# A decoder layer on one core: first weight halves in quarters, retention queries and keys from x without its norm, x through ScalarE's queue

## What is computed

```python
h = rms_norm(x, attn_norm)                       # x * rsqrt(mean(x*x)) * gain
q_r, k_r, v_r, g_r, q_m, k_m, v_m = split(h @ w_in)
qr, kr = rotary(q_r, pos), rotary(k_r, pos)      # cos and sin per position and channel
o_r = retention_chunkwise(qr, kr, v_r)           # scores * decay, then values
... # group norm, MoBA attention, gates, output projection, residual, norm, gated MLP with a convolution
```

## Time and profile before

| | us |
|---|---|
| median of 3 runs (lowest, highest) | 477.55 (477.21, 477.62) |
| the profiled execution | 477.05 |
| its span, first to last instruction | 475.3 |
| TensorE busy in it | 468.3 |
| VectorE busy in it | 300.1 |
| ScalarE busy in it | 254.4 |

### The profile page before, as it was taken

One profiled execution on the slowest core, in us unless ns is written; L12 is line 12 of the kernel. 1 busy time (PEld: TensorE's weight loads), 2 busy tenths in 40 slices (PEclk: granted clock), 3 DMA queues, 4 the chain that ended last, 5 costly groups with the idle time before them and its releaser, 6 DMA issues.

```text
span 475.3 us, 7781 instructions
## 1 busy us (share of the span) xinstructions
PE 468.3 (99%) x3117; PEld 431.4 (91%) x3117; DVE 300.1 (63%) x364; ACT 254.4 (54%) x362; POOL 19.6 (4%) x27
## 2 busy tenths in 40 slices
PE   7999999999999999999999999999999999999997
PEld 5789999888888999999999888999999999988885
DVE  4787882755664637355338676687777878885312
ACT  5774432147774849224445355776666666663400
POOL 0300000311110001000000000000000000000000
DMA  8997444254445525753443733615554555538002
GB/s 299 413 375 266 178 177 179 90 182 166 150 147 220 199 88 178 311 177 134 157 188 122 267 145 132 248 67 223 187 185 189 183 193 187 196 123 329 1 1 88
DMA packets 13979, 87.20 MB, mean 183 GB/s; under 512 B 1537, under 2 KB 1921, under 8 KB 4353
## 3 DMA queue, kind: packets, MB, share of 16 engines
q1 hardware_dynamic: 13536, 85.25, 48.0%
q0 software_dynamic: 416, 1.57, 0.8%
HBM read 85.77 MB, written 1.05 MB: 183 GB/s over the span
## 4 chain that ended last, share of the span: by engine, by line
PE 94%; DMA 3%; SPq 1%; POOL 1%; issue 0%; DVE 0%; ACT 0%; POOLq 0%
PE bank L365 18%; PE bank L366 18%; PE bank L367 18%; PE bank L331 5%; PE bank L329 5%; PE bank L330 5%; PE bank L601 4%; PE bank L602 4%; PE bank L604 4%; DMA ys<-x_dram 3%; PE bank L518 2%; PE bank L520 2%; PE bank L519 2%; PE bank L384 2%; PE bank L467 1%; PE bank L449 1%
## 5 line engine op out<-in xcount | busy, mean ns | idle before, releaser
L900 DVE TENSOR_TENSOR w_lo<-w_raw,w_hi 128x2048 fp32r<-128x2048 f32 x75 | 170.4, 2288 | 78.7 <-ACT w_hi L624 78.4
L365 PE MATMUL bank<-h_hi,w_hi 128*128 128x256 f32 x576 | 163.8, 284 | 0.0
L366 PE MATMUL bank<-h_lo,w_hi 128*128 128x256 f32 x576 | 163.0, 283 | 0.0
L367 PE MATMUL bank<-h_hi,w_lo 128*128 128x256 f32 x576 | 163.0, 283 | 0.0
L624 ACT ACTIVATE w_hi<-w_raw 128x2048 fp32r<-128x2048 f32 x75 | 141.7, 1914 | 31.5 <-PE bank L604 16.9
L365 PEld LDWEIGHTS bank<-h_hi,w_hi 128*128 128x128 f32 x576 | 110.5, 192 | 0.5 <-issue 0.4
L366 PEld LDWEIGHTS bank<-h_lo,w_hi 128*128 128x128 f32 x576 | 110.6, 192 | 0.1
L367 PEld LDWEIGHTS bank<-h_hi,w_lo 128*128 128x128 f32 x576 | 110.5, 192 | 0.0
L1162 DVE SCALAR_TENSOR_TENSOR area<-area,col 128x256 f32<-128x256 f32 x88 | 37.8, 481 | 19.9 <-ACT area L827 17.3
L329 PE MATMUL bank<-w_hi,h_hi 128*128 128x512 f32 x96 | 37.9, 395 | 0.0
L331 PE MATMUL bank<-w_hi,h_lo 128*128 128x512 f32 x96 | 37.4, 390 | 0.0
(11 more groups left out here) (132 smaller groups left out, 559.8 us busy)
## 6 DMA issues: line engine op xcount, KB each, us to landing
w_raw<-weights_dram SPq DMA_DIRECT2D x75, 1024.0 KB, 4.8
w_raw<-weights_dram SPq DMA_DIRECT2D x3, 512.0 KB, 7.1
ys<-x_dram SPq DMA_DIRECT2D x2, 512.0 KB, 12.5
xs<-x_dram POOLq DMA_DIRECT2D x1, 1024.0 KB, 7.8
out_dram<-ys SPq DMA_DIRECT2D x4, 256.0 KB, 2.0
area<-decay_dram SPq DMA_DIRECT2D x1, 768.0 KB, 13.2
w_raw<-weights_dram SPq DMA_DIRECT2D x2, 256.0 KB, 4.3
xs<-x_chan_dram SPq DMA_DIRECT2D x1, 512.0 KB, 6.3
```

The lines of the kernel that those rows point to most:

```text
L365: mm(o, s_hi, r_hi[:, k, :], start=(k == 0 and m % 2 == 0), stop=False)
L366: mm(o, s_hi, r_lo[:, k, :], start=False, stop=False)
L367: ins = mm(o, s_lo, r_hi[:, k, :], start=False, stop=(k == KT - 1 and m % 2 == 1))
L900: tt(w_lo[r][:, :], raw[r][:, :], w_hi[r][:, :].bitcast(f32), ALU.subtract).then_inc(lo_ready, 1)
```

## The change

- Halves 2 and 3 are loaded in two pieces each and split in four quarters on ScalarE and VectorE, and TensorE waits for each quarter in V_R1 as well.
- The three `x_chan` transfers are issued by ScalarE, ahead of its table load, in place of SyncE.
- SyncE issues the two token tiles of x between halves 2 and 3; `ident` goes last.
- ScalarE squares both token tiles, after half 2; VectorE squares none.
- Q_R and K_R are computed from `xg`. VectorE multiplies the two rotary tables by inv (`scale_tables`, two instructions of 128 x 256), where `normalise` was. `normalise` and `h_high` move one block later (`second[V_R1]`), and G_R0 is the first block to wait for `h_ready`. `rotate` takes `ys` for scratch.

```diff
--- before.py
+++ after.py
@@ -138,7 +138,7 @@
         bank = [ctx.enter_context(nc.psum_tensor(f"bank{i}", [P, 512], f32)) for i in range(8)]
 
         raw_loaded = [sem(f"raw_loaded{r}") for r in range(SLOTS)]
-        raw_start = [sem(f"raw_start{i}") for i in range(3)]
+        raw_start = [sem(f"raw_start{i}") for i in range(SLOTS + 1)]
         x_chan_loaded = [sem(f"x_chan_loaded{c}") for c in range(3)]
         xg_hi_ready = sem("xg_hi_ready")
         xg_lo_ready = sem("xg_lo_ready")
@@ -218,27 +218,20 @@
 
         @block.sync
         def _(sp):
-            def load_x_chan(c, piece, k0, k1):
-                a, z = 2 * KT + SEQ * k0 if k0 else 0, 2 * KT + SEQ * k1
-                sp.dma_start(x_head[:, a:z], piece).then_inc(x_chan_loaded[c], 16)
-
             def load_quarters(r, q0, q1, done):
                 part = slice(512 * q0, 512 * q1)
                 sp.dma_start(raw[r][:, part], weights[r, :, part]).then_inc(done, 16)
 
             load_quarters(0, 0, 1, raw_start[0])
-            load_x_chan(0, x_chan0, 0, 2)
             load_quarters(0, 1, 2, raw_start[1])
-            load_x_chan(1, x_chan1, 2, 4)
             load_quarters(0, 2, 4, raw_loaded[0])
-            load_x_chan(2, x_chan2, 4, KT)
-            load_quarters(1, 0, 2, raw_start[2])
-            load_quarters(1, 2, 4, raw_loaded[1])
-            for r in range(2, SLOTS):
-                sp.dma_start(raw[r][:, :], weights[r]).then_inc(raw_loaded[r], 16)
+            for r in range(1, SLOTS):
+                load_quarters(r, 0, 2, raw_start[r + 1])
+                load_quarters(r, 2, 4, raw_loaded[r])
+                if r == 2:
+                    for t in range(NT):
+                        sp.dma_start(y_tok[:, t, :], x_view[:, t, :]).then_inc(x_loaded[t], 16)
             sp.dma_start(ident[:, :], ident_in).then_inc(ident_loaded, 16)
-            for t in range(NT):
-                sp.dma_start(y_tok[:, t, :], x_view[:, t, :]).then_inc(x_loaded[t], 16)
             for r in range(SLOTS):
                 sp.wait_ge(lo_ready, r + 1)
                 sp.dma_start(raw[r][:, :], weights[SLOTS + r]).then_inc(raw_loaded[r], 16)
@@ -337,18 +330,19 @@
 
                     def quarter_split(kk):
 
-                        pe.wait_ge(xg_lo_ready, 4 * h + kk + 1)
+                        if b == V_R0:
+                            pe.wait_ge(xg_lo_ready, 4 * h + kk + 1)
                         if kk < 3:
                             pe.wait_ge(piece_lo, 3 * n + kk + 1)
                         else:
                             pe.wait_ge(lo_ready, n + 1)
 
-                    if b > 0:
+                    if b > V_R1:
                         pe.wait_ge(lo_ready, n + 1)
                     if h == 0:
                         wait_bank_free(b)
                     token_half([block_bank(b, t) for t in range(NT)], n, range(4 * h, 4 * h + 4), h == 0, h == 1,
-                               before=quarter_split if b == 0 else None, src=src).then_inc(half_used, 1)
+                               before=quarter_split if b <= V_R1 else None, src=src).then_inc(half_used, 1)
                     if b == V_R1 and h == 0:
                         inv_rows()
 
@@ -371,7 +365,7 @@
                 for h in range(2):
                     n = 2 * b + h
                     pe.wait_ge(lo_ready, n + 1)
-                    if b == Q_R:
+                    if b == G_R0:
                         pe.wait_ge(h_ready, h + 1)
                     if h == 0:
                         wait_bank_free(b)
@@ -471,8 +465,8 @@
 
             token_block(V_R0, (xg_hi, xg_lo))
             token_block(V_R1, (xg_hi, xg_lo))
-            channel_block(Q_R, h_hi, h_lo)
-            channel_block(K_R, h_hi, h_lo)
+            channel_block(Q_R, xg_hi, xg_lo)
+            channel_block(K_R, xg_hi, xg_lo)
             channel_block(G_R0, h_hi, h_lo)
             tail_ret_scores()
             channel_block(G_R1, h_hi, h_lo)
@@ -613,6 +607,9 @@
         def _(act):
             A = nc.scalar.activation
 
+            for c, (piece, k0, k1) in enumerate(((x_chan0, 0, 2), (x_chan1, 2, 4), (x_chan2, 4, KT))):
+                a, z = 2 * KT + SEQ * k0 if k0 else 0, 2 * KT + SEQ * k1
+                act.dma_start(x_head[:, a:z], piece).then_inc(x_chan_loaded[c], 16)
             nc.scalar.preload_act_table(ACT.Square)
 
             def split(n, r=None, count=None):
@@ -627,7 +624,7 @@
                 if q == 2:
                     act.wait_ge(raw_loaded[n], 16)
                 elif q == 0 or (n, q) == (0, 1):
-                    act.wait_ge(raw_start[2 * n + q], 16)
+                    act.wait_ge(raw_start[n + 1 if n else q], 16)
                 c = slice(512 * q, 512 * q + 512)
                 A(w_hi[n][:, c], raw[n][:, c], ACT.Copy).then_inc(piece_hi, 1)
 
@@ -641,10 +638,13 @@
                 xg_high(k)
                 if k:
                     split_quarter(k // 4, k % 4)
-            split(2)
-            act.wait_ge(x_loaded[0], 16)
-            A(square_out, y_tok[:, 0, :], ACT.Square, accum_out=ss_x[:, 0:1]).then_inc(sums_x[0], 1)
-            split(3)
+            for q in range(4):
+                split_quarter(2, q)
+            for t, scratch in enumerate((square_out, square_out2)):
+                act.wait_ge(x_loaded[t], 16)
+                A(scratch, y_tok[:, t, :], ACT.Square, accum_out=ss_x[:, t:t + 1]).then_inc(sums_x[t], 1)
+            for q in range(4):
+                split_quarter(3, q)
 
             def copy_block(b, dst):
                 for t in range(NT):
@@ -787,7 +787,7 @@
                 MOBA_O0: lambda: merged_high(MOBA_O0), MOBA_O1: lambda: merged_high(MOBA_O1),
             }
             second = {
-                V_R0: lambda: (scale_block(V_R0, lambda t: v_r[:, t, 0:512]), h_high()),
+                V_R0: lambda: scale_block(V_R0, lambda t: v_r[:, t, 0:512]), V_R1: h_high,
                 Q_M1: lambda: ret_read(0), K_M0: lambda: ret_read(1),
                 V_M1: lambda: exps(0),
                 GATE_R0: lambda: sigmoid_gates(GATE_R0, GATE_R0, 0),
@@ -896,7 +896,7 @@
             def split(n, r=None):
 
                 r = n % SLOTS if r is None else r
-                dve.wait_ge(hi_ready, n - 1)
+                dve.wait_ge(hi_ready, n - 3)
                 tt(w_lo[r][:, :], raw[r][:, :], w_hi[r][:, :].bitcast(f32), ALU.subtract).then_inc(lo_ready, 1)
 
             def split_quarter(n, q):
@@ -910,10 +910,18 @@
                 stt(out=xg_lo[:, k, :], in0=x_t[:, k, :], scalar=gain_col[:, k:k + 1], in1=xg_hi[:, k, :].bitcast(f32),
                     op0=ALU.mult, op1=ALU.subtract).then_inc(xg_lo_ready, 1)
 
-            def normalise():
+            def scale_tables():
 
                 u = unit("inv_row", 0)
                 dve.wait_ge(unit_made, u + 1)
+                dve.wait_ge(rotary_loaded, 16)
+                for table in (cos_t, sin_t):
+                    ins = tt(table, table, ubank(u)[:, 0:SEQ], ALU.mult)
+                step(ins)
+
+            def normalise():
+
+                u = unit("inv_row", 0)
 
                 def low(kh):
                     k = slice(4 * kh, 4 * kh + 4)
@@ -928,6 +936,7 @@
                 ins.then_inc(unit_read[u % 4], 1)
                 low(0)
                 low(1)
+                dve.wait_ge(h_ready, 2)
 
             nc.vector.memset(w_lo[SLOTS - 1][:, 0:512].bitcast(f32), 0.0).then_inc(zeros_ready, 1)
             split_quarter(0, 0)
@@ -937,21 +946,17 @@
                 xg_low(k)
                 if k:
                     split_quarter(k // 4, k % 4)
-            split(2)
-            dve.wait_ge(x_loaded[1], 16)
-            nc.vector.tensor_tensor_reduce(out=square_out2, in0=y_tok[:, 1, :], in1=y_tok[:, 1, :], scale=1.0,
-                                           scalar=0.0, op0=ALU.mult, op1=ALU.add,
-                                           accum_out=ss_x[:, 1:2]).then_inc(sums_x[1], 1)
-            dve.wait_ge(warm_done, 1)
-            split(3)
+            for n in (2, 3):
+                if n == 3:
+                    dve.wait_ge(warm_done, 1)
+                for q in range(4):
+                    split_quarter(n, q)
 
             def rotate(b):
 
                 dve.wait_ge(half_used, 2 * b + 2)
-                if b == Q_R:
-                    dve.wait_ge(rotary_loaded, 16)
                 half = RET_QK // 2
-                tmp = xs[:, 0:512].rearrange("p (h s) -> p h s", h=2)
+                tmp = ys[:, 0:512].rearrange("p (h s) -> p h s", h=2)
 
                 def spread(table, a, z):
                     return table[a:z, :].unsqueeze(1).broadcast_to([z - a, 2, SEQ])
@@ -1120,7 +1125,7 @@
                 MOBA_O0: lambda: gate_moba(MOBA_O0), MOBA_O1: lambda: gate_moba(MOBA_O1),
             }
             second = {
-                V_R0: normalise,
+                V_R0: scale_tables, V_R1: normalise,
                 G_R1: group_norm,
```

2 lines of the change are left out of this document (1 added, 1 removed).

## The result

The changed kernel takes 478.3 us (median of 12 runs, 478.1 to 479.6), the kernel before 477.5 us (median of 12 runs). The ratio is 1.0023 with a 95% interval of 1.0015 to 1.0031; it is estimated from all the runs, and the two medians alone would give 1.0016. So the kernel is slower, clear of noise, by far less than 2%. The forecast was 476.1 us, so even the sign was wrong. Eight of the twelve runs lie between 478.1 and 478.4 us and four between 479.2 and 479.6, and the profiled execution, at 478.26 us with a span of 476.5 us, is one of the eight.

What follows compares the result with a forecast made beforehand. TensorE was taken as the bound (work in 468.3 of 475.3 us), so only its idle time could be gained: 0.83 + 0.11 + 0.31 + 0.19 = 1.44 us, from 477.55 to 476.1 us; range 475.7 to 477.9.

Steps and rivals of the forecast that it cites:

- The order in which x and weights arrive: Start of the kernel: x on ScalarE's queue gains and costs nothing if pairs keep their order; called the open question.
- the first rival: At the start, weights land with or behind x (5.5 and 9.4 us): gain only 0.1 us, 477.4 us; chance 0.35.
- starting issues sooner brings nothing: Early transfers of x and weights: bound by bytes at some 400 GB/s, so earlier issue gives no gain.
- The slower rival: At the start, x goes through whole, first weight lands 2.5 us later: 478.6 us, 480.7 with slow products; chance 0.10.
- The sum is 1.44 us: TensorE waits removed: 0.83 and 0.11 at half 2, 0.31 at the spread of inv, 0.19 at Q_R.
- ScalarE's three issues: Ahead of ScalarE's table load: 1.3 us for three issues of x, covered by idle time, so no cost.
- Token tiles, GpSimd, half 3: Before the spread: tiles land earlier, GpSimd's second chain ends by 22.5 us, the inv wait goes (0.31 us), half 3 in time.
- `scale_tables`: VectorE between the splits of halves 4 and 5: 0.8 us for two instructions, hidden, no cost.
- VectorE late for half 8: Near 52.5 us: moved `normalise` uses up the 0.5 us margin before half 8, giving 476.6 us; chance 0.08.
- The range: Median from 475.7 us to 477.9 us, leaving out the case of starving weights.

Runs made afterwards that it cites:

- x_on_sync: Changed kernel with the three channel pieces of x back on SyncE's queue in their old places: 476.4 us, ratio 0.9980.
- before_x_act: Kernel before with only the three channel pieces of x moved to ScalarE's queue: 478.3 us, ratio 1.0022.
- after_warm19: Changed kernel with 19 warm-up products in place of 9: 477.6 us, ratio 1.0002.
- norm_earlier: x_on_sync with normalised x formed right behind the scaled rotary tables, its low parts ahead of half 6's split: 475.9 us, ratio 0.9969.
- before_late: Kernel before with 17 warm-up products in place of 9, so TensorE's first real product starts later: 477.4 us, ratio 1.0000.
- quarters_only: x_on_sync with Q_R and K_R computed from normalised x again and the norm where it was before: 477.7 us, ratio 1.0006.
- xg_only: Kernel before with only Q_R and K_R from `xg`, the norm placed as in norm_earlier: 477.3 us, ratio 0.9997.
- ident_act_first: x_on_sync with the 64 KB identity matrix issued by ScalarE at the start instead of by SyncE at the end: 476.4 us, ratio 0.9980.

## Why the prediction was wrong, step by step

**The order in which x and weights arrive.** This is the step that failed. The forecast let x go to a second queue at no cost, "if pairs keep their order". They did not. The first weight quarter landed at 6.27 us in place of 4.83, the second half of half 0 at 10.06 in place of 8.10, and TensorE began 1.41 us late. Behind its idle time the first products ran at the slow pace, which cost another 1.50. So TensorE was 2.91 us late at its thirteenth product, caught up 1.67 by Q_R, and stayed 1.24 behind where the forecast had it 1.44 ahead. That x's queue is the cause is shown from both sides: with x back on SyncE's queue the changed kernel takes 1.9 us less (x_on_sync), and with x moved and nothing else the kernel before takes 0.8 us more (before_x_act). The queues shared about evenly, which is the first rival's mechanism. Its times were too small, 5.5 and 9.4 us for the two weight pieces; two queues moved 170 GB/s from 2 to 5 us where one moved 224. The prediction's sentence that starting issues sooner brings nothing held: x's first piece, issued at 0.73 us, took 5.7 us to land in place of 4.3. The rule in the Trainium skill, "Trainium Kernel Development and Optimization", section Key Constraints, that a second issuing engine saves issue time alone, was right so far as it goes and too kind here: 1.9 us were lost by it. The packet-wise alternation of "DMA: Bandwidth & Descriptors" (the Trainium skill, section Queues, rings and completion order) does not settle which data comes first; the even split of the two queues is what the trace shows.

**The slower rival.** It was given 0.10, as "weights starve", with the point of decision at a first weight more than 1.44 us late. It was late by just that, without x having gone first. The rival's plain price was for a weight 2.5 us late, and the slow pace stood beside it as an extra for that case alone. Here both were paid, 1.41 us and 1.50 us, and without the second the kernel would not have been slower: after_warm19, whose first products run at full pace, takes what the kernel before takes (477.6 against 477.5). Two rivals whose prices belong to one mechanism, the late weight, should have been one: sharing by 0.65 us or more, together with a first stretch that may be slow.

**"The sum is 1.44 us".** As the worth of all parts together, for a kernel whose first product is on time, this held: in x_on_sync Q_R starts at 29.68 us in place of 30.79, and norm_earlier, where the wait for half 8 is gone too, is 1.5 us below the kernel before. The changed kernel can't show it, since its late start takes the same waits away by itself (before_x_act). What was wrong is what the sum says of its terms. The distances in the earlier trace rows were read rightly, but each was called the gain of one part, as if it were TensorE's own. They are lids in a row, set by the transfers: half 2 (18.71), the token tiles through GpSimd (24.59), half 4 through VectorE's order (30.79). Behind such a row the last one decides. A start 1.4 us later is free (before_late), removing the first two waits is worth nothing (quarters_only), and removing the third gives 0.1 (xg_only). This did not make the forecast miss; it made the expectation of quarters_only miss, and it is why the same late start costs 0.8 us in the kernel before and 1.9 in the changed one.

**ScalarE's three issues.** 1.4 us in place of 1.3, and hidden: right. They held up the table load, as it was expected, and nothing waited for that.

**Token tiles, GpSimd, half 3.** Right: inv was ready at 20.4 us (forecast 22.5 at worst), and no wait before or behind the spread.

**`scale_tables`.** 0.74 us, hidden: right.

**VectorE late for half 8.** The mechanism was right, the margin of 0.5 us was mis-sized by 1.2: half 6's split on ScalarE stood behind half 5's and the read of V_R1, which the chain of terms left out. In the changed kernel this lid doesn't bite, as TensorE is late itself; with x on SyncE's queue it takes 0.77 us.

**The range.** 475.7 to 477.9 was bounded by the first rival plus spread. Since that rival's own price was too small and had no slow stretch in it, the upper end was too low by 0.4 us.

## What to carry to other kernels

Where an engine waits several times in a row for things that don't depend on it, don't add the waits: work out for each stage the earliest time at which each of its inputs can be there, and take the latest; a gain is worth what is left at the last one. A second DMA queue was not free at the start of this kernel, even if its issues were: what it carried took bandwidth from the one piece that everybody waits for, so put large early transfers in one queue in the order of need. Where no lid is left, the start shows at the end. Three more warm-up products, which end just ahead of the first real one, are then cheap to try: here they gave 475.7 us in place of 475.9, which the intervals do not tell apart.

## What the hardware showed beyond that

- At the start of the program two queues with most of x on the second moved less than one: 163 to 181 GB/s from 2 to 5 us in five profiled executions, against 211 to 233 with one queue, one execution with 140 aside. Why is open; 64 KB on the second queue cost nothing in the median.
- The pace of TensorE's first products varies between executions with nine warm-up products. After 2.6 us of idle time or more all four profiled executions had slow products, seven to fourteen of them about 0.43 us apart. After less it went both ways: slow behind 0.83, 0.88 and 1.36 us (quarters_only, norm_earlier, ident_act_first), full pace behind 1.00, 1.10 and 1.25 us (the kernel before, xg_only, x_on_sync). So the length of the idle time alone does not decide it, and what does is open. The granted clock is printed as 1.00 in one slow stretch (norm_earlier) and as 0.57 in another (changed kernel), so the distance of the starts is the row to trust. The Trainium skill, "TensorE: Matmul & The Clock Gate", section Seeing it yourself, warns that the recorded clock events are unreliable on this chip; the stretch of norm_earlier bears that out.
- In the kernel before such a slow start would hardly show in the time, since a start 1.4 us later did not (before_late).
- A DMA issue written behind an activation table load on ScalarE does not wait for it (0.76 us against the load's end at 2.0).
